# Six residual rows kept in the output early, and the last layer's rows added onto them by adding transfers

## The reference, cut to what matters

```
x = x + gt1[:, None, :] * rms_norm(m, g_post1)
h = modulate(rms_norm(x, g_pre2), sh2, sc2)
f = peer_ffn(h, w_q, sub_keys, u_tab, v_tab)
x = x + gt2[:, None, :] * rms_norm(f, g_post2)      # y_prompt, y_sample
```

## Time and profile before

| | us |
|---|---|
| median of three runs | 1742.88 |
| the three runs | 1744.26, 1734.13, 1742.88 |
| the profiled execution, its time | 1733.52 |
| its span, first to last instruction | 1731.7 |
| TensorE busy in it | 1708.8 |
| VectorE busy | 1049.7 |
| GpSimd busy | 1051.5 |
| ScalarE busy | 557.6 |

### The profile page before, as it was taken

How to read it: one execution, slowest core, us unless ns; L and a number is a source line. 1 busy time by engine, 2 the same in 40 slices (tenths; PEclk the granted TensorE clock), 3 DMA queues, 4 the chain that set the end, 5 groups by cost and what they waited for, 6 DMA issues and landing times.

```text
span 1731.7 us, 31304 instructions
## 1 busy us (share of the span) xinstructions
PE 1708.8 (99%) x12782; PEld 1675.1 (97%) x12782; DVE 1049.7 (61%) x2187; ACT 557.6 (32%) x754; POOL 1051.5 (61%) x706
## 2 busy tenths in 40 slices
PE   8999999999999999999999999999999999999997
PEld 6999879799999999999999999999999999999996
DVE  5624473765776457676632222226888889888884
ACT  4122144432333323232322222223333333333332
POOL 0430100028878888888888888866777788766501
PEclk9999999999999999999999999999999999999998
DMA  9989352623666665757576666669999999999961
GB/s 369 385 290 324 121 207 98 235 95 38 130 145 133 128 143 107 157 112 150 127 155 149 134 143 135 142 170 363 364 386 399 380 361 352 375 366 365 370 245 50
DMA packets 191415, 385.20 MB, mean 222 GB/s; under 512 B 73352, under 2 KB 131144, under 8 KB 176424
## 3 DMA queue, kind: packets, MB, share of 16 engines
q1 hardware_dynamic: 110760, 306.47, 51.3%
q0 software_dynamic: 80512, 76.74, 20.1%
HBM read 318.44 MB, written 64.19 MB: 221 GB/s over the span
## 4 chain that ended last, share of the span: by engine, by line
PE 79%; DVE 1%; DMA 1%; ACT 0%; issue 0%; SPq 0%; DVEq 0%; ACTq 0%
PE ps L1724 42%; PE ps L1748 30%; PE ps L625 5%; PE ps L1698 1%; DMA ahead_dram<-a 1%; DVE h L2079 0%; ACT qp L1854 0%; PE ps L1708 0%; PE ps L1762 0%; PE ps L871 0%; DVE x L2086 0%; DVE ul L1939 0%; PE ps L1781 0%; ACT uh L1790 0%; PE ps L579 0%
## 5 line engine op out<-in xcount | busy, mean ns | idle before, releaser
L101 POOL DMA_INDIRECT gates_dram<-gate,where x384 | 644.7, 1679 | 191.1 <-issue 178.5
L1724 PE MATMUL ps<-hh,ul 128*128 128x260 f32 x2048 | 413.2, 283 | 0.0
L1724 PE MATMUL ps<-hl,uh 128*128 128x260 f32 x2048 | 413.2, 283 | 0.0
L1724 PE MATMUL ps<-hh,uh 128*128 128x260 f32 x2048 | 412.4, 283 | 0.0
L1939 DVE TENSOR_TENSOR ul<-us,uh 128x1024 fp32r<-128x1024 f32 x132 | 161.1, 1221 | 349.5 <-ACT uh L1790 345.0
L1748 PE MATMUL ps<-cl,uh 128*128 128x384 f32 (+1 forms) x1024 | 345.1, 337 | 0.7 <-DVE ul L1939 0.7
L1748 PE MATMUL ps<-ch,ul 128*128 128x384 f32 x1024 | 344.4, 336 | 0.0
L1748 PE MATMUL ps<-ch,uh 128*128 128x384 f32 x1024 | 344.4, 336 | 0.0
L1724 PEld LDWEIGHTS ps<-hl,uh 128*128 128x128 f32 x2048 | 315.6, 189 | 0.4 <-issue 0.4
L1724 PEld LDWEIGHTS ps<-hh,ul 128*128 128x128 f32 x2048 | 315.8, 189 | 0.0
L1724 PEld LDWEIGHTS ps<-hh,uh 128*128 128x128 f32 x2048 | 314.8, 188 | 0.0
(11 more groups left out here) (251 smaller groups left out, 2145.7 us busy)
## 6 DMA issues: line engine op xcount, KB each, us to landing
us<-utab SPq DMA_DIRECT2D x128, 512.0 KB, 3.9
pairs<-vtab SPq DMA_DIRECT2D x62, 1024.0 KB, 8.3
gates_dram<-blank SPq DMA_DIRECT2D x24, 1024.0 KB, 11.9
ahead_dram<-a SPq DMA_DIRECT2D x128, 192.0 KB
qp<-ahead_dram SPq DMA_DIRECT2D x32, 768.0 KB, 7.0
gt<-gates_dram SPq DMA_DIRECT2D x32, 768.0 KB, 9.5
wr<-w_ada SPq DMA_DIRECT2D x20, 1024.0 KB, 5.1
wr<-w_in SPq DMA_DIRECT2D x14, 1024.0 KB, 9.2
```

Source lines behind the costliest of these rows:

```text
L101: nc.gpsimd.indirect_dma_start(out=io["gates"].rearrange("g p c a t -> (g p c a t)").unsqueeze(1), out_offset=bass.IndirectOffsetOnAxis(ap ...
L1724: last = nc.tensor.matmul(out[:, half, :], w, r[:, k, half * TH:(half + 1) * TH], start=(k == 0 and q == 0), stop=(k == KD - 1 and q == 2))
```

## The change

Rows 0 to 5 (`SUMMED = 6`) of the prompt's columns are written from `x` to `yT` in the first stage, at m = 64 of SyncE's loop (`x_kept`). In the tail GpSimd issues for each of them, once it is scaled, a transfer of `acc` to `yT` with an addition (`accum_op`), and waits for all six at the end. The samples' columns of these rows go in a transfer of their own. VectorE adds rows 6 and 7, GpSimd none.

```diff
-        ON_POOL = (0, 2, 4)
+        SUMMED = 6
...
@@ sync_program, first stage
+                if m == NK // 2:
+                    for k in range(SUMMED):
+                        sp.dma_start(io["yT"][:, k, 0:SEQ], x[:, k, 0:SEQ]).then_inc(x_kept, 16)
...
-            for k in range(KD):
-                if k in ON_POOL:
-                    sp.wait_ge(yp_ok, ON_POOL.index(k) + 1)
-                else:
-                    sp.wait_ge(y_ok, k + 1 - len([n for n in ON_POOL if n < k]))
+            sp.wait_ge(y_ok, 1)
+            sp.dma_start(io["yT"][:, 0:SUMMED, SEQ:T], x[:, 0:SUMMED, SEQ:T]).then_inc(y_out, 16)
+            for k in range(SUMMED, KD):
+                sp.wait_ge(y_ok, k - SUMMED + 2)
                 sp.dma_start(io["yT"][:, k], x[:, k]).then_inc(y_out, 16)
-            sp.wait_ge(y_out, 16 * KD)
+            sp.wait_ge(y_out, 16 * (KD - SUMMED + 1))
...
@@ gpsimd_program, end
-            for n, k in enumerate(ON_POOL):
+            pool.wait_ge(x_kept, 16 * SUMMED)
+            for k in range(SUMMED):
                 pool.wait_ge(t_ok, k + 1)
-                nc.gpsimd.tensor_tensor(x[:, k, 0:SEQ], x[:, k, 0:SEQ], acc[:, k, 0:SEQ], ALU.add).then_inc(yp_ok, 1)
-            pool.wait_ge(yp_ok, len(ON_POOL))
+                pool.dma_start(io["yT"][:, k, 0:SEQ], acc[:, k, 0:SEQ], accum_op=ALU.add).then_inc(y_summed, 16)
+            pool.wait_ge(y_summed, 16 * SUMMED)
...
@@ vector_program, end
-            nc.vector.tensor_tensor(x[:, :, SEQ:T], x[:, :, SEQ:T], tsm[:], ALU.add)
+            nc.vector.tensor_tensor(x[:, :, SEQ:T], x[:, :, SEQ:T], tsm[:], ALU.add).then_inc(y_ok, 1)
...
             def added(k):
 
-                if k in ON_POOL:
-                    return
                 dve.wait_ge(t_ok, k + 1)
                 nc.vector.tensor_tensor(x[:, k, 0:SEQ], x[:, k, 0:SEQ], acc[:, k, 0:SEQ], ALU.add).then_inc(y_ok, 1)
 
             for k in range(KD):
                 scaled(k)
-                if k:
+                if k > SUMMED:
                     added(k - 1)
             added(KD - 1)
```

More of the change, by code:

```diff
@@ L1582, in peer_stage @@
         y_ok = sem("y_ok")
-        yp_ok = sem("yp_ok")
+        x_kept = sem("x_kept")
+        y_summed = sem("y_summed")
         y_out = sem("y_out")
```

## The result

Twelve runs of the changed kernel gave a median of 1756.8 us (1748.52 to 1759.69), twelve of the one before 1741.09 us (1733.61 to 1757.82). The ratio is 1.0066 with a 95% interval of 1.0043 to 1.0089: slower by some 11 us, less than 1% and clear of no change. The prediction had 1742.7 us, a gain of 0.15 us. The profiled execution took 1752.46 us for a span of 1750.6.

The account below looks back on a forecast made before the run. TensorE bounds the stages; VectorE's chain and the output transfers bound the tail. VectorE's 1.8 us gain, nearly all given back by adding transfers, left 0.15 us: 1742.88 - 0.15 = 1742.7 us, range 1732 to 1750.

Parts of the forecast that it names:

- What ends the span: Tail: the last output transfer lands at 1729.8 us and 1.9 us of closing waits follow; GpSimd's additions are hidden.
- GpSimd's closing wait behind the adding transfers: End of the tail: GpSimd's final wait for its six adding transfers, given no cost of its own.
- The landing of the last adding transfer: Tail: lands 4.9 us after its issue starts, at 1729.65 us, giving back nearly all of VectorE's 1.8 us.
- How much the engines move: DMA engines in the tail: six rows take 3.7 us, or 7.5 us even where each takes twice as long.
- the second rival: Tail: adding rows need two reads per write, 1.25 us each per DMA engine; +1.2 us, 1744.1 us, chance 0.21.
- Two reads for each write: Tail: reduction in the DMA path halves the rate, six rows taking 7.5 us; +1.2 us, 1744.1 us, chance 0.21.
- Issue on GpSimd: Tail: GpSimd issues the six adding transfers 0.85 us apart, the last starting at 1724.75 us.
- VectorE's side: Tail: VectorE adds two rows in place of five, ending at 1725.9 us, a gain of 1.8 us.
- The six rows kept early: First stage, about 798 us: six early transfers take 2.3 us of SyncE's queue and cost nothing in time.

Follow-up runs that it names:

- `pool_held`: The kernel before, with GpSimd also waiting for SyncE's eight output transfers after its three additions; 1738.45 us against 1733.33, ratio 1.0031.
- `two_on_pool`: The kernel before, with GpSimd adding rows 0 and 2 and VectorE six rows, no adding transfers; 1732.68 us against 1733.33, ratio 0.9994.
- the square: Changed kernel with plain or adding transfers, last wait on SyncE or GpSimd; tails 11.4 and 14.5 us plain, 18.9 and 21.3 us adding.
- `after_again`: The changed kernel once more, without edit, on the same chip as the other experiments; 1742.42 us against 1733.29 before, ratio 1.0050.
- `kept_only`: The kernel before, plus the early writes of six rows at m = 64 and the wait for them; 1733.74 us against 1733.29, ratio 1.0004.
- `none_on_pool`: The kernel before, with all eight additions on VectorE and plain transfers from SyncE; one run, 1737.47 us, tail 12.2 us.

## Why the prediction was wrong, point by point

- *What ends the span* ("1.9 us of closing waits follow the last landing"; GpSimd's additions "are hidden"): this step failed first. The 1.9 us were not a constant after SyncE but the end of GpSimd's DRAIN: 5.7 us of issue and additions after the first scaled row's start, then 6.0 us. GpSimd was on the path that sets the end, hidden from the busy lines because a DRAIN isn't counted as busy. In the changed kernel 7.0 us follow the last landing. `pool_held` shows it (4.7 us for a wait alone), `two_on_pool` from the other side.
- *GpSimd's closing wait behind the adding transfers*: costed at nothing. It moves the start of the DRAIN from 5.7 us of the tail to 15.4, or 14.6 in the second profile. By the square the place of the wait is worth 2.4 to 3.1 us.
- *The landing of the last adding transfer* (4.9 us from its issue, range 2.9 to 5.9): it was up to 11.2 us. The high end of the range was too low, since I bounded a transfer by itself and left out that six of them share the engines. I had worked out that term in "How much the engines move" and the second rival, with 1.25 us for a row on each engine; measured 27.5 / 16 = 1.72 us. Six rows at that rate fill the engines for 10.3 us. This term decided, and stood among the rivals only.
- *Two reads for each write*, from the Trainium skill ("Collectives: The Full Stack", "The bandwidth ceiling: the fold count and why AG ≠ RS ≠ AR"): an adding transfer is slower, as the page has it for ReduceScatter, and the factor 2 is less than the 2.5 measured for six transfers at a time, 2.1 for one of 1.5 MB (24 against 11.2). That two reads are the cause here isn't shown.
- *Issue on GpSimd* (0.85 us apart): the starts are 0.57 us apart (1729.6 to 1732.5 over five steps), the ends 0.9, as each issue takes longer than the one before: 0.99 to 2.67 us. A plain one takes 0.57. Right in size, without consequence.
- *VectorE's side*: right. Eight multiplications and two additions end 6.1 us into the tail instead of 8.0. The gain of 1.9 us is there and reaches nobody.
- *The six rows kept early*: right that it costs nothing, off in the details. The load of block 64 is that of 785.60 before (786.01 changed), not 797.79; I was three loads off. The six issues held SyncE's queue for 4.1 us instead of 2.3. ScalarE's longest wait for `keep` grew from 7.8 to 10.6 us, and TensorE still had no gap.

The chances had 0.93 within 1%, and the time did fall there; the range of 1732 to 1750 missed. That the 1% held is no merit of the sum, whose direction was wrong. Its upper end lacked the DRAIN (about 5 us) and the shared engines. The tail's 9.3 to 10.2 us lie inside the interval of both timings (7.5 to 15.5 us, and 6.2 to 11.3 us). The medians of the first timing are 15.7 us apart and its first profile lost 8.7 us ahead of the tail, with TensorE idle in places and a mean granted clock of 0.89 and 0.77 in 1340 to 1345 and 1345 to 1350. `after_again` had neither. Why the stages were longer there stays open; `kept_only` only excludes the early writes as a cause that shows on its chip, and `none_on_pool` has such a loss without them.

## What to carry to other kernels

At a program's end ask of each engine when its last instruction ends and what its closing costs, and look at the uncounted instructions for it: here GpSimd needs 6 us after its last wait, so its work belongs at the front of the tail and a wait for output on another engine. An adding transfer isn't a free addition: it took 2.1 to 2.5 times the DMA engines' time of a plain one, and where it is the last thing of a kernel, that is exposed, with every plain transfer queued beside it. The version with the shortest tail measured moves one addition from GpSimd to VectorE, though VectorE was on the chain shown; its gain of 0.8 us in the profile is too small for the timed runs (ratio 0.9994, 0.9982 to 1.0005), so that it is cheaper than before isn't shown.

## What the runs showed of the hardware that I had not expected

GpSimd's closing DRAIN took 6.03 us with no transfer of its own in the tail, 6.52 us after six transfers that had landed and been waited for, and 6.11 after one. Started while GpSimd was still issuing, it lasted 7.2, 9.5, 10.4 and 14.7 us (six plain, two, three and six adding transfers), and 8.3 us behind the gathers in `none_on_pool`; after the six adding ones it ended 3.1 us behind the moment at which SyncE saw them land. The DRAINs of SyncE took 0.007 us and that of VectorE 1.2 us.
